# The first unit's lanes with a step per half block, and layer two's first chunk without its meta tokens from the output projection on

## The chip, the cores and the metric

One core of a Trainium2 chip runs the whole program. The metric is the device time of one execution in microseconds. Engines are named as in the profile: PE (TensorE), DVE (VectorE), ACT (ScalarE), POOL (GpSimd) and SP (the queue that issues the loads). Everything is computed in f32.

## The reference

Two layers over 16 meta tokens and 1024 tokens, width 1024. Cut to what matters here:

```python
h = layer_norm(concat([meta, x]))
for i in range(2):
    p_conv, p_swa, p_ret, p_rwkv = split(h @ w_in[i])
    mix = concat([short_conv(p_conv), swa(p_swa), retention(p_ret), rwkv7(p_rwkv)]) @ w_out[i]
    h = layer_norm(ALPHA * h + mix)                      # first norm
    z = causal_dwconv(h @ ffn_w_up[i], ffn_conv_w[i])    # three taps
    u, gate = split(z)
    h = layer_norm(ALPHA * h + (silu(gate) * u) @ ffn_w_down[i])   # second norm
return h[:, N_META:]                                     # the 16 meta tokens are dropped
```

The mixers carry state from the meta tokens to all that follow: attention reads their keys and values in every window, retention and RWKV carry a state. After the mixers of layer two nothing reads the meta tokens but the causal convolution of the feed-forward part, whose three taps reach two tokens back.

## The kernel before

The 1040 tokens are cut into four chunks, the first of 272 tokens (16 meta tokens and 256), the others of 256. A unit u is one chunk in one layer: units 0 to 3 are layer one, 4 to 7 layer two. `chunk_of(u)` gives a unit's first token and its width. Activations are kept transposed, features on partitions and tokens along the free dimension, so the width of a unit is the number of columns of each of its dense products.

A unit has 25 input blocks (`dense`, L852: one weight slot, eight products of 128x128 weights by the unit's columns, summed in one of two PSUM banks that blocks use in turn), 8 output blocks, 44 up blocks and 8 down sums of 22 products each (L1294). PE waits in `bank_free` (L835) until the block two before has been read out by ACT (`evac`) or DVE. SP loads the 792 weight slots of 512 KB in the order of use, five slots deep, each when the slot's last use is over.

Each engine has its own program, written out in Python generators that are advanced in one and the same order on all of them. `alongside(main, *sides)` makes one step of the main program and then one step of each lane; `yield` ends a step. So what stands in a lane's step is issued behind the main part of that step on every engine, and an engine works strictly in its program order. The lanes of a unit are `rwkv(u)` (transposes, scores, a triangular inverse in levels, where PE, DVE's mask at L1708 and ACT's copy at L662 alternate, then the state by tiles) and `side(u)` (retention by tiles with its norm, then sliding-window attention by tiles). From unit 1 on the lanes run beside the up and down products of the unit before. Unit 0 has no unit before it: its lanes run beside its own last input blocks and beside the eight retention input blocks of unit 1 (`project_retention(1)`), and the output projection of unit 0 (`mixer_out(0)`) waits for both lanes. The constants at L112 say after how many steps of the main program the lanes start: RWKV after 12, the input norms of tiles 3 and 4 after 21, retention after 28, attention after 57. In this stretch every block from the 13th on has three steps, of three, three and two products (`steps_after` (2, 5)).

Unit 0's input blocks come in the order of `input_part(0)`: RWKV's seven, retention's eight, the convolution's six, attention's four (sq0, sq1, sk, sv). Two extra products turn sq0, sq1 and sk for the rotary part (tq0, tq1, tk); DVE finishes them in `rotate_swa` and then fills the windows kbuf and vbuf, after which the lane's attention may start. `short_conv` on DVE (L1472 to L1485) runs once cb0 and cb1 are read out.

In retention DVE makes a reciprocal over 544 columns (L1778) and two products. In attention DVE scales and masks the scores (L1793), takes the maximum, ACT makes four exponentials (L733), DVE divides (L1812), PE transposes (L841), ACT copies, PE multiplies by the values (L1239).

The norms of a unit (`residual`, `ln_center`, `ln_normalize` on DVE, `ln_squares`, `ln_affine` on ACT, `ln_mean`, `ln_var` on PE) run beside the blocks of the next unit and have the unit's width.

Of the kernel before, what the change touches and what calls it, by code (L numbers as in the profile page):

```python
# [13 lines left out]
P = 128  # L14
KD = D // P
# [3 lines left out]
HD = 64  # L19
# [51 lines left out]
def input_part(u):  # L71

    return MIX_PART + ([] if u == 1 else RET_PART) + CONV_PART + SWA_PART
# [38 lines left out]
RWKV_START, INPUT_START, SIDE_START, ATTENTION_START = 12, 21, 28, 57  # L112
# [162 lines left out]
def build(nc, x, meta, weights, params, ln_in, ln_rows, consts, tables, out):  # L275
    with ExitStack() as ctx:
# [231 lines left out]
        def _(a):  # L508
            act = a.activation

            def evac(u, name, dst, func=ACT.Copy, bias=None, parts=P):
                i, n = AT[u, name], chunk_of(u)[1]
# [19 lines left out]
            def ln_squares(i):  # L532
                t0, n = chunk_of(i // 2)
# [7 lines left out]
            def ln_affine(i):  # L541
                u, ph = divmod(i, 2)
                t0, n = chunk_of(u)
# [12 lines left out]
            def project(u):  # L556
# [16 lines left out]
                for i, name in enumerate(input_part(u)):  # L573
                    if u == 0 and i >= RWKV_START:
                        yield
                        yield
# [4 lines left out]
                    if u and i == 10:  # L581
                        evac(u - 1, "var1", rstdT[:, :chunk_of(u - 1)[1]], ACT.Sqrt, eps_ln)
# [43 lines left out]
            def project_retention(u):  # L626
# [3 lines left out]
                for name in RET_PART:  # L630
                    yield
                    yield
# [8 lines left out]
            def rwkv(u):  # L641
                for gi, group in enumerate(groups_of(u)):
# [12 lines left out]
                    if u:  # L655
                        yield
# [38 lines left out]
                if u:  # L695
                    yield
# [7 lines left out]
            def side(u):  # L704
# [23 lines left out]
                for i, (j, off, n_) in enumerate(tiles):  # L728
# [8 lines left out]
                    if u:  # L737
                        yield
# [22 lines left out]
            def ffn(u):  # L761
                n = chunk_of(u)[1]
# [17 lines left out]
            def last_norms(u):  # L780
# [5 lines left out]
                evac(u, "var2", rstdT[:, :chunk_of(u)[1]], ACT.Sqrt, eps_ln)  # L786
# [17 lines left out]
            for u in range(NU - 1):  # L804
                if u:
                    rest(ln_squares(2 * u - 1))
                    evac(u - 1, "var2", rstdT[:, :chunk_of(u - 1)[1]], ACT.Sqrt, eps_ln)
# [8 lines left out]
            evac(last, "var1", rstdT[:, :chunk_of(last)[1]], ACT.Sqrt, eps_ln)  # L816
# [8 lines left out]
        def _(pe):  # L825
# [17 lines left out]
            def feature(u, name, pairs, steps_after=()):  # L843
                i, n = AT[u, name], chunk_of(u)[1]
# [23 lines left out]
            def ln_mean(i):  # L868
                u, ph = divmod(i, 2)
                pe.wait_ge(S["dm_sum"], 7 * nth_norm(i) + 7)  # L870
                rest(feature(u, f"mean{ph + 1}", [(c("mean"), xsum[:, nth_norm(i) % 2, :chunk_of(u)[1]])]))

            def ln_var(i):
                u, ph = divmod(i, 2)
                pe.wait_ge(S["ln_sqs"], 7 * nth_norm(i) + 7)
                rest(feature(u, f"var{ph + 1}", [(c("mean"), sqsum[:, :chunk_of(u)[1]])]))
# [19 lines left out]
            def project(u):  # L896
# [12 lines left out]
                for i, name in enumerate(input_part(u)):  # L909
# [7 lines left out]
                    yield from dense(u, name, h, (2, 5) if u == 0 and i >= RWKV_START else ())  # L917
# [103 lines left out]
            def rwkv(u):  # L1021
                first = 1 + ROW["lo"]
                pe.wait_ge(S["smallV"], SMALL_FREED[u, "bo1"])
                for gi, group in enumerate(groups_of(u)):
# [46 lines left out]
                    if u:  # L1071
                        yield
# [1000 lines left out]
```

## Time and profile before

| | |
|---|---|
| median of 3 runs | 3317.38 us (3315.71 to 3317.96) |
| the profiled execution's own time | 3317.04 us |
| its span, first to last instruction | 3315.1 us |
| mean granted clock of TensorE | 0.995 |
| PE busy | 3259.3 us (98%) |
| DVE / ACT / POOL busy | 1346.4 / 867.0 / 34.2 us |
| read from HBM | 427.27 MB, 130 GB/s over the span |

Busy time of PE is that of its matmul records; PEld is the load of weights, which lies beside them. An f32 product is two records. An idle time in the timeline stands in brackets ahead of a group, with what ended it. A granted clock of 1.00 is TensorE's 2.4 GHz, and a stretch's value is a mean over time at either level.

### The profile page before, as it was taken

To read this page: it belongs to the slowest core of one execution; us is meant where nothing else is said; L and a number is where in the kernel's file an instruction comes from. 1 tells how busy PE (TensorE), PEld (TensorE's weight loads), DVE (VectorE), ACT (ScalarE), POOL (GpSimd) and SP (SyncE) were. 2 spreads that over 40 slices of the span, in tenths; PEclk is the share of its full clock that TensorE was granted. 3 is DMA by queue.
4 is the path that set the end of the run, shared out by engine and by line. 5 is a ranking of instruction groups with operands and counts; after the bars stand their busy time and mean duration, and the time that the engine had idled before them with its cause. 6 is when DMAs were issued, how large, how long until landed. Compare 5 with 4: busy or idle time off the path is not lost.

```text
span 3315.1 us, 51403 instructions
## 1 busy us (share of the span) xinstructions
PE 3259.3 (98%) x21648; PEld 2740.6 (83%) x21648; DVE 1346.4 (41%) x3184; ACT 867.0 (26%) x2561; POOL 34.2 (1%) x47
## 2 busy tenths in 40 slices
PE   8989999999999999999999999999999999999998
PEld 6768788888888888878888887888888888888887
DVE  4334452345524454153541534415354153542541
ACT  3223340123402242032330324203242042311320
POOL 0000000000000000000000000000000000000000
PEclk9999999999999999999999999999999999999999
DMA  6134234443344434443334432444334443344443
GB/s 198 58 100 139 91 116 146 147 139 96 127 153 147 134 97 140 153 140 128 103 115 153 140 121 97 140 142 139 127 104 157 149 138 116 121 153 162 154 155 115
DMA packets 128867, 434.79 MB, mean 131 GB/s; under 512 B 13296, under 2 KB 25712, under 8 KB 128384
## 3 DMA queue, kind: packets, MB, share of 16 engines
q1 hardware_dynamic: 127488, 427.32, 39.8%
q8 instruction: 172, 2.82, 0.3%
q0 software_dynamic: 1152, 4.19, 0.3%
q14 instruction: 55, 0.45, 0.0%
HBM read 427.27 MB, written 4.19 MB: 130 GB/s over the span
## 4 chain that ended last, share of the span: by engine, by line
PE 96%; DVE 2%; ACT 1%; issue 0%; DMA 0%; SPq 0%; POOL 0%; DVEq 0%; ACTq 0%
PE psum L847 66%; PE psum L1294 19%; PE psum L841 2%; PE psum L861 2%; PE psum L1095 1%; PE psum L1108 1%; PE psum L1128 1%; PE psum L1239 1%; PE psum L1111 1%; PE psum L1051 0%; PE psum L1221 0%; PE psum L1191 0%; PE psum L1194 0%; DMA con<-in_consts 0%; PE psum L1009 0%
## 5 line engine op out<-in xcount | busy, mean ns | idle before, releaser
L847 PE MATMUL psum<-hT,slots 128*128 128x256 f32 (+1 forms) x8832 | 2012.2, 386 | 11.3 <-DMA con<-in_consts 2.9
L847 PEld LDWEIGHTS psum<-hT,slots 128*128 128x128 f32 x8832 | 1661.6, 190 | 294.1 <-issue 40.5
L1294 PE MATMUL psum<-gT,slots 128*128 128x256 f32 (+1 forms) x2816 | 620.1, 382 | 0.3 <-DVE hT L1398 0.2
L1294 PEld LDWEIGHTS psum<-gT,slots 128*128 128x128 f32 x2816 | 534.3, 190 | 82.7 <-issue 0.5
L1398 DVE SCALAR_TENSOR_TENSOR hT<-hT,psum 128x256 f32<-128x256 f32 (+1 forms) x128 | 54.4, 425 | 622.7 <-PE psum L1294 509.2
L773 ACT ACTIVATE last<-psum 128x2 f32<-128x2 f32 x352 | 60.2, 171 | 910.1 <-PE psum L847 910.0
L847 PE MATMUL psum<-mixT,slots 128*128 128x256 f32 (+1 forms) x1024 | 228.6, 383 | 2.0 <-DVE hT L1398 1.4
L847 PEld LDWEIGHTS psum<-mixT,slots 128*128 128x128 f32 x1024 | 193.6, 190 | 35.8 <-issue 6.6
L1859 DVE TENSOR_SCALAR tmpG<-raw,par 128x256 f32<-128x256 f32 (+1 forms) x176 | 62.7, 356 | 383.4 <-ACT raw L774 383.3
L538 ACT ACTIVATE scr<-hT 128x256 f32<-128x256 f32 (+1 forms) x120 | 47.8, 420 | 593.0 <-DVE hT L1417 569.4
L1859 DVE TENSOR_SCALAR gT<-raw,par 128x256 f32<-128x256 f32 (+1 forms) x176 | 62.4, 355 | 329.1 <-ACT raw L774 329.0
L774 ACT ACTIVATE raw<-psum 128x256 f32<-128x256 f32 (+1 forms) x352 | 134.4, 382 | 0.0
L1863 DVE SCALAR_TENSOR_TENSOR tmpG<-raw,par,tmpG 128x256 f32<-128x256 f32 (+1 forms) x176 | 86.8, 493 | 6.3
L1861 DVE SCALAR_TENSOR_TENSOR tmpG<-raw,par,tmpG 128x256 f32<-128x256 f32 (+1 forms) x176 | 86.8, 493 | 6.3
L1863 DVE SCALAR_TENSOR_TENSOR gT<-raw,par,gT 128x256 f32<-128x256 f32 (+1 forms) x176 | 86.1, 489 | 6.3
L1861 DVE SCALAR_TENSOR_TENSOR gT<-raw,par,gT 128x256 f32<-128x256 f32 (+1 forms) x176 | 86.0, 489 | 6.2
L515 ACT ACTIVATE rows<-psum 128x256 f32<-128x256 f32 (+1 forms) x80 | 31.0, 387 | 218.0 <-PE psum L847 218.0
L1458 DVE TENSOR_TENSOR gT<-rows 128x256 f32<-128x256 f32 (+1 forms) x56 | 24.1, 430 | 137.1 <-ACT rows L565 115.1
L766 ACT ACTIVATE tmpG<-tmpG 128x256 f32<-128x256 f32 (+1 forms) x176 | 74.1, 421 | 12.8 <-DVE tmpG L1863 12.4
L1853 DVE TENSOR_TENSOR gT<-gT,tmpG 128x256 f32<-128x256 f32 (+1 forms) x176 | 74.3, 422 | 1.2
L547 ACT ACTIVATE hT<-hT,par 128x256 f32<-128x256 f32 (+1 forms) x120 | 60.9, 591 | 41.8 <-DVE hT L1437 41.8
L1607 DVE TENSOR_TENSOR rows<-rows,tab 128x256 f32<-128x256 f32 (+1 forms) x48 | 20.5, 426 | 107.0 <-PE psum L847 76.3
(246 smaller groups left out, 2388.0 us busy)
## 6 DMA issues: line engine op xcount, KB each, us to landing
slots<-in_weights SPq DMA_DIRECT2D x792, 512.0 KB, 3.4
hT<-in_x SPq DMA_DIRECT2D x8, 512.0 KB, 5.3
out<-prpt POOLq DMA_DIRECT2D x8, 512.0 KB, 3.0
tab<-in_tables SPq DMA_DIRECT2D x6, 512.0 KB, 4.6
con<-in_consts SPq DMA_DIRECT2D x1, 1562.0 KB, 10.6
tab<-in_tables SPq DMA_DIRECT2D x2, 544.0 KB, 5.7
mixT<-in_ln_rows SPq DMA_DIRECT2D x1, 1024.0 KB, 7.1
par<-in_params SPq DMA_DIRECT2D x2, 386.5 KB, 5.4
```

What stands on the lines that cost most here:

```text
L547: act(hT[:, m, t0:t0 + n], hT[:, m, t0:t0 + n], ACT.Identity, bias=gb[:, KD + m:KD + m + 1], scale=gb[:, m:m + 1]).then_inc(S["ln_hT"], 1)
L766: act(tmpG[:, m % 2, :n], tmpG[:, m % 2, :n], ACT.Silu).then_inc(S["g_silu"], 1)
L773: act(last2[:, u % 2, f, :], psum[:, i % 2, n - 2:n], ACT.Copy)
L774: act(buf[:, 2:2 + n], psum[:, i % 2, :n], ACT.Copy).then_inc(S["evA"], 1)
L841: return pe.transpose(dst, src, ident[:n, :n])
L847: ins = mm(psum[:, i % 2, :n], lhsT, rhs, start=k == 0, stop=k == len(pairs) - 1)
L861: ins = mm(psum[:parts, b, :n], lhsT, rhs, start=k == 0, stop=k == len(pairs) - 1)
L1294: ins = mm(psum[:, i % 2, :n], w[:, e * P:(e + 1) * P], gT[:, k, :n], start=k == 0, stop=k == KF - 1)
L1853: tt(gT[:, m, :n], gT[:, m, :n], tmpG[:, m % 2, :n], ALU.mult).then_inc(S["glu"], 1)
L1859: k = step(ts(y, src[:, 2:2 + n], par[:, w + 2:w + 3], None, ALU.mult))
L1861: k = step(stt(y, src[:, 1:1 + n], par[:, w + 1:w + 2], y, ALU.mult, ALU.add))
L1863: stt(y, src[:, 0:n], par[:, w:w + 1], y, ALU.mult, ALU.add).then_inc(S["fconv"], 1)
```

## The change

`span_of(u, ph)` gives the tokens of a unit that the work after the mixers covers, for the first norm (ph 0) and the second (ph 1). It is the whole chunk but for unit 4, layer two's first: there 14 of the 16 meta tokens are left out from the output projection to the up projection (258 columns remain), all 16 in the down projection and second norm (256). `width(u, name)` picks the width of a block by its name.

In unit 0 the input order becomes RWKV, retention, attention, convolution; tq1 and tk and the filling of the windows follow sv at once instead of standing at the end. A block from the 13th on has two steps of four products each instead of three, in unit 0 and in `project_retention(1)`. The four start constants become 12, 14, 18, 30. Lane steps that only units from 1 on had (`if u: yield`, three places on each engine) unit 0 now has too, one more ahead of RWKV's S2 scores in each of its two groups, one ahead of its last transposes, and one between attention's scores and its transposed probabilities in each tile. In units from 1 on the order of instructions stays as it was.

```diff
+def span_of(u, ph):
+    t0, n = chunk_of(u)
+    skip = (META if ph else META - 2) if u == NCH else 0
+    return t0 + skip, n - skip
+
+def width(u, name):
+    if name[:3] == "out" or name[:2] == "up" or name in ("mean1", "var1"):
+        return span_of(u, 0)[1]
+    return span_of(u, 1)[1] if name[:2] == "dn" or name in ("mean2", "var2") else chunk_of(u)[1]
@@ def input_part(u):
+    if u == 0:
+        return MIX_PART + RET_PART + SWA_PART + CONV_PART
     return MIX_PART + ([] if u == 1 else RET_PART) + CONV_PART + SWA_PART
@@
-RWKV_START, INPUT_START, SIDE_START, ATTENTION_START = 12, 21, 28, 57
+RWKV_START, INPUT_START, SIDE_START, ATTENTION_START = 12, 14, 18, 30
@@ tensor: def project(u)
-                    yield from dense(u, name, h, (2, 5) if u == 0 and i >= RWKV_START else ())
+                    yield from dense(u, name, h, (3,) if u == 0 and i >= RWKV_START else ())
...
-                    yield
-                pe.wait_ge(S["evA"], FREED[AT[u, "sk"]])
-                rest(feature(u, "tq1", [(c("permS"), row("sq1", n))]))
-                rest(feature(u, "tk", [(c("permS"), temp("sk", n))]))
+                    if name == "sv":
+                        pe.wait_ge(S["evA"], FREED[AT[u, "sk"]])
+                        rest(feature(u, "tq1", [(c("permS"), row("sq1", n))]))
+                        rest(feature(u, "tk", [(c("permS"), temp("sk", n))]))
+                    yield
                 yield
@@ tensor: def project_retention(u)
-                    yield from dense(u, name, h_of(u), (2, 5))
+                    yield from dense(u, name, h_of(u), (3,))
@@ tensor, scalar, vector: rwkv(u), side(u)
-                    if u:
-                        yield
+                    yield
@@ scalar, vector: project(u), project_retention(u): one yield less for each block
-                        yield
@@ tensor: def mixer_out(u)
+                first = span_of(u, 0)[0] - chunk_of(u)[0]
-                    rest(dense(u, f"out{m}", [mixT[:, k, :n] for k in range(KD)]))
+                    rest(dense(u, f"out{m}", [mixT[:, k, first:n] for k in range(KD)]))
@@ tensor: def up(u)
-                h = h_of(u)
+                t0, n = span_of(u, 0)
+                h = [hT[:, k, t0:t0 + n] for k in range(KD)]
@@ tensor: def down(u)
-                n = chunk_of(u)[1]
+                n = span_of(u, 1)[1]
+                first = span_of(u, 0)[1] - n
...
-                        ins = mm(psum[:, i % 2, :n], w[:, e * P:(e + 1) * P], gT[:, k, :n], start=k == 0, stop=k == KF - 1)
+                        ins = mm(psum[:, i % 2, :n], w[:, e * P:(e + 1) * P], gT[:, k, first:first + n], start=k == 0, stop=k == KF - 1)
@@ vector: def project(u): rotations and windows
-                    yield
-                rotate_swa(1, row("sq1", n), "tq1")
-                rotate_swa(2, temp("sk", n), "tk")
-                read_out(u, "sv")
...
+                        rotate_swa(1, row("sq1", n), "tq1")
+                        rotate_swa(2, temp("sk", n), "tk")
+                        read_out(u, "sv")
...
@@ residual, ln_center, ln_normalize, ln_squares, ln_affine, ln_mean, ln_var, ffn, up
-                t0, n = chunk_of(u)
+                t0, n = span_of(u, ph)
```

## Rows read from the trace of the kernel before

**Rows 1.** first lines of the page: busy time, share and instructions of each engine

```profile
PE 3259.3 (98%) x21648; PEld 2740.6 (83%) x21648; DVE 1346.4 (41%) x3184; ACT 867.0 (26%) x2561; POOL 34.2 (1%) x47
...
PE psum L847 66%; PE psum L1294 19%; PE psum L841 2%; PE psum L861 2%; PE psum L1095 1%; PE psum L1108 1%; PE psum L1128 1%; PE psum L1239 1%; PE psum L1111 1%; PE psum L1051 0%; PE psum L1221 0%; PE psum L1191 0%; PE psum L1194 0%; DMA con<-in_consts 0%; PE psum L1009 0%
```

**Rows 2.** two stretches of dense work: PE, PEld, DVE, ACT, POOL busy (instructions), clock, DMA

```profile
550.00:600.00 50.00, 50.00 (x220) 41.44 (x219) 4.41 (x10) 0.00 (x0) 0.00 (x0) 1.00 0.44 140
...
1350.00:1400.00 50.00, 50.00 (x233) 44.01 (x233) 4.23 (x10) 0.00 (x0) 0.00 (x0) 1.00 0.50 156
```

**Rows 3.** instruction groups by shape: busy us, mean ns, idle before

```profile
L1294 PE MATMUL psum<-gT,slots 128*128 128x272 f32 x704 | 161.7, 392 | 0.0
...
L847 PE MATMUL psum<-mixT,slots 128*128 128x272 f32 x256 | 59.5, 393 | 0.4 <-DVE hT L1398 0.4
...
L1294 PEld LDWEIGHTS psum<-gT,slots 128*128 128x128 f32 x2816 | 534.3, 190 | 82.7 <-issue 0.5 <-DVE hT L1398 0.5
```

**Rows 4.** waits of PE in 0 to 260 us: total, times, longest

```profile
PE psum L841 <- DVE prpt L1812: 8.5, 3, 4.0
...
PE psum L847 <- DVE gT L1608: 1.6, 2, 1.1
...
PE psum L1095 <- POOL wset L484: 1.4, 1, 1.4
```

**Rows 5.** the first unit's lanes as one window, columns as in group 2

```profile
70.00:230.00 160.00, 141.91 (x1556) 108.56 (x1556) 54.90 (x138) 46.83 (x123) 4.09 (x6) 0.94 0.23 73
```

**Rows 6.** PE in order of time: start us, us, group, idle before

```profile
94.32 1.97 PE L841 MATMUL psum<-con,hT 128*128 128x128 f32 x8 [1.62 <-DVE hT L1381]
...
96.08 4.60 PE L847 MATMUL psum<-hT,slots 128*128 128x272 f32 x10
...
130.51 1.15 PE L1095 MATMUL psum<-wset 64*64 64x64 f32 x32
...
158.71 0.37 PE L1009 MATMUL psum<-Zb,wset 64*64 64x64 f32 x2 [2.92 <-DVE Zb L1665]
...
159.76 4.90 PE L847 MATMUL psum<-hT,slots 128*128 128x272 f32 x10
...
198.84 0.97 PE L1221 MATMUL psum<-kbuf,rows 64*128 64x208 f32 x8
...
199.75 2.42 PE L847 MATMUL psum<-hT,slots 128*128 128x256 f32 x10
...
206.19 1.97 PE L841 MATMUL psum<-con,prpt 128*128 128x128 f32 x8 [4.02 <-DVE prpt L1812]
```

**Rows 7.** VectorE in order of time

```profile
112.59 0.69 DVE L1708 TENSOR_TENSOR wset<-psum,con 128x512 f32<-128x512 f32 x1 [2.82 <-PE psum L1095]
...
149.52 0.06 DVE L1472 MEMSET rows<- 128x2 f32 x1 [8.94 <-ACT gT L515]
...
151.56 0.44 DVE L1485 TENSOR_TENSOR mixT<-mixT,gT 128x272 f32<-128x272 f32 x1
...
153.40 3.54 DVE L1778 RECIPROCAL prpt<-prpt 128x544 f32<-128x544 f32 x1
...
157.73 0.72 DVE L1782 TENSOR_TENSOR mixT<-mixT,prpt 128x544 f32<-128x544 f32 x1
...
178.61 0.50 DVE L1742 SCALAR_TENSOR_TENSOR mixT<-mixT,par,rows 128x272 f32<-128x272 f32 x1 [1.44 <-ACT mixT L699]
...
180.10 0.50 DVE L1744 SCALAR_TENSOR_TENSOR mixT<-mixT,par,rows 128x272 f32<-128x272 f32 x1
...
199.86 1.02 DVE L1793 SCALAR_TENSOR_TENSOR SC<-psum,con 128x832 f32<-128x832 f32 x1 [4.48 <-PE psum L1221]
```

**Rows 8.** ScalarE in order of time

```profile
90.17 1.28 ACT L520 ACT_TABLE_LOAD   x1
...
91.47 0.29 ACT L520 ACTIVATE small<-small,con 128x1 f32<-128x1 f32 x1
...
96.33 2.90 ACT L527 ACTIVATE hT<-psum,ln_in_cols 128x128 f32<-128x128 f32 x8 [3.31 <-PE psum L841]
```

More of the change, by code:

```diff
@@ L581, in project @@
                     if u and i == 10:
-                        evac(u - 1, "var1", rstdT[:, :chunk_of(u - 1)[1]], ACT.Sqrt, eps_ln)
+                        evac(u - 1, "var1", rstdT[:, :span_of(u - 1, 0)[1]], ACT.Sqrt, eps_ln)
                     if name in MIX_PART:
@@ L736, in side @@
                     yield
-                    if u:
-                        yield
+                    yield
                     a.wait_ge(S["a_pt"], nth + 1)
@@ L785, in last_norms @@
                     yield
-                evac(u, "var2", rstdT[:, :chunk_of(u)[1]], ACT.Sqrt, eps_ln)
+                evac(u, "var2", rstdT[:, :span_of(u, 1)[1]], ACT.Sqrt, eps_ln)
                 yield
@@ L806, in _ @@
                     rest(ln_squares(2 * u - 1))
-                    evac(u - 1, "var2", rstdT[:, :chunk_of(u - 1)[1]], ACT.Sqrt, eps_ln)
+                    evac(u - 1, "var2", rstdT[:, :span_of(u - 1, 1)[1]], ACT.Sqrt, eps_ln)
                     ln_affine(2 * u - 1)
@@ L815, in _ @@
             rest(ln_squares(2 * last))
-            evac(last, "var1", rstdT[:, :chunk_of(last)[1]], ACT.Sqrt, eps_ln)
+            evac(last, "var1", rstdT[:, :span_of(last, 0)[1]], ACT.Sqrt, eps_ln)
             ln_affine(2 * last)
@@ L870, in ln_mean @@
                 pe.wait_ge(S["dm_sum"], 7 * nth_norm(i) + 7)
-                rest(feature(u, f"mean{ph + 1}", [(c("mean"), xsum[:, nth_norm(i) % 2, :chunk_of(u)[1]])]))
+                rest(feature(u, f"mean{ph + 1}", [(c("mean"), xsum[:, nth_norm(i) % 2, :span_of(u, ph)[1]])]))
             def ln_var(i):
@@ L875, in ln_var @@
                 pe.wait_ge(S["ln_sqs"], 7 * nth_norm(i) + 7)
-                rest(feature(u, f"var{ph + 1}", [(c("mean"), sqsum[:, :chunk_of(u)[1]])]))
+                rest(feature(u, f"var{ph + 1}", [(c("mean"), sqsum[:, :span_of(u, ph)[1]])]))
             def input_tile(j):
@@ L1070, in rwkv @@
                     yield
-                    if u:
-                        yield
+                    yield
                     pe.wait_ge(S["w_t0"], nth + 1)
@@ L1136, in rwkv @@
                 yield
-                if u:
-                    yield
+                yield
                 pe.wait_ge(S["w_norm"], u + 1)
@@ L1225, in side @@
                     yield
-                    if u:
-                        yield
+                    yield
                     pe.wait_ge(S["a_pn"], nth + 1)
@@ L1560, in project @@
                         yield
-                        yield
                     if i == 2:
@@ L1585, in project @@
                         rotate_swa(0, row("sq0", n), "tq0")
[L1586 to L1596 removed]
+                        rotate_swa(1, row("sq1", n), "tq1")
+                        rotate_swa(2, temp("sk", n), "tk")
+                        read_out(u, "sv")
+                        v.wait_ge(S["a_rope"], 3 * u + 3)
+                        k = step(v.tensor_copy(kbuf[:, :, KPAD:], temp("sk", n)[:, first:].rearrange("p (b s) -> p b s", b=2)))
+                        if c0:
+                            k = step(v.tensor_copy(kbuf[:, :, 0:META], temp("sk", n)[:, None, 0:META].broadcast_to([P, 2, META])))
+                        after(k)
+                        v.tensor_copy(kbuf[:, 1, META:KPAD], kbuf[:, 0, WIN - HD:])
+                        v.tensor_copy(vbuf[:, 1, META:KPAD], vbuf[:, 0, WIN - HD:]).then_inc(S["a_window"], 1)
+                    yield
                 yield
@@ L1697, in rwkv @@
                     yield
-                    if u:
-                        yield
+                    yield
                     v.wait_ge(S["w_s2"], g_ + 1)
@@ L1734, in rwkv @@
                 yield
-                if u:
-                    yield
+                yield
                 yield
@@ L1814, in side @@
                     yield
-                    if u:
-                        yield
+                    yield
                     yield
```

25 lines of the change are left out of this document (8 added, 17 removed).

## The prediction

> **What bounds the kernel now.** I read the engine totals first: PE is busy 98% of the span of 3315.1 us, VectorE (DVE) 41% and ScalarE (ACT) 26%, and the chain that ended last lies mostly on PE's dense products [rows 1]. So time goes away in two ways only: fewer columns through PE, or less time in which PE waits or runs at the lower clock. Next the dense stretches: 50 us hold 220 matmul records of 272 columns or 233 of 256 [rows 2], 0.2273 and 0.2146 us each (an f32 product is two records; a block of eight products is 16). PE is never idle there. Last the waits of PE: after the start-up there is one stretch with many of them, the lanes of unit 0 (70 to 230 us), where PE is busy 141.91 of 160 us, so idle 18.1, at a mean clock of 0.94 [rows 5]. Its largest entries are attention waiting for the normalized probabilities (8.5 us in three waits), rotated features (1.6) and POOL's mask (1.4) [rows 4], the state step (2.9) and the input tile (1.6) [rows 6]. All else that the two parts touch lies in PE's dense stretches.
>
> **Part A, unit 4 without its meta tokens.** Output projection, first norm and up projection go from 272 to 258 columns, down projection and second norm to 256. Counts: of the 256 mixT records of 272 columns half are unit 4's, 128; of the 704 gT records half, 352 [rows 3]; the up projection has 44 blocks x 16 = 704. A column of a record costs (0.2273 - 0.2146)/16 = 0.00079 us [rows 2]. Down: 352 x 0.0127 = 4.5. Output and up: 832 x 14 x 0.00079 = 9.2. Mean and variance products: 8 records, 0.1. Sum 13.8; I take 14.0, since one record more or less in a window of 50 us moves the sum by about 1, so 12.8 to 15. No block of 258 columns is in the trace: its pace lies between that of 256 and of 272 columns, so those 832 records give between 0 and 10.6 us, and I take the linear 9.2, because PE's pace is the same share of the columns at both widths. Narrower operations on DVE and ACT hide under PE and save nothing; a shorter block also shortens the cover of the lanes there, by 6%, and DVE at about half busy has room. The weight queue must bring a slot in 3.43 instead of 3.64 us, which it does in every stretch of 256 columns without a wait of PE [rows 2].
>
> A weight load takes 190 ns [rows 3] and the pace at 256 columns is 214.6 ns. The Trainium skill, TensorE: Matmul & The Clock Gate, section Back-to-back issue gap, says that the spacing of a stream is set by weight load and matmul together. If the load set it, part A would give nothing; the two paces of [rows 2] differ by the columns, so the trace speaks against this here.
>
> **Part B, unit 0's lanes.** A lane advances by one step at each yield of the main program. Before, blocks from the 13th on have three yields, afterwards two: a step then has half a block, 1.96 us at 272 columns or 1.7 to 1.8 at 256, instead of about 1.2 (a block is 16 x 0.2273 = 3.64 us by [rows 2], somewhat more with lane work between). PE's work is the same. I counted lane steps of after as calls 1 to 55 (76 before). RWKV: calls 13 to 53, its first group 13 to 24, second group's transposes 26, scores 27, levels 30 to 39, tiles 41 to 48, last transposes 52. Other lane: input tiles 15 to 18, retention 19 to 29, attention 31 to 46. In before retention and attention lay apart, at 29 to 40 and 58 to 70, attention alone at the end. Now each wait.
>
> Attention. Score products end at 199.8, the chain SC, max, four exponentials and division ends at 206.2, 6.4 us, and PE has 10 records (2.4 us) to do meanwhile [rows 6]. Now it gets three steps instead of two, 5.4 to 5.9 us, with an RWKV step of 1 to 2 us in each. The chain is covered, also with 0.7 us of another lane's DVE work in it [rows 7]: 8.5 us go.
>
> State step. The wait of 2.9 us is DVE's reciprocal (3.54) with its two products, 153.4 to 158.4 [rows 7], queued ahead of the state addition. It moves with retention to call 29, behind the S2 masks. DVE then reaches the mask of the first level 4.9 + 0.7 us after them; PE has two half blocks and one level product (1.15 [rows 6]) from 1.4 us before them on: 1.4 + 4.9 + 0.7 - 3.9 - 1.15 = 1.9 us late. So 2.9 and the 1.0 beside it become 1.9.
>
> Rotated features. They now come in calls 24 to 26 with DVE free, so nearly all of 1.6 goes; 0.2 stays for tk behind ScalarE's copy of sv. The rotations and copies (5 us on DVE) stand ahead of retention's mask, but PE has 16 transposes, retention scores, a half block and the RWKV scores before it needs that: no wait.
>
> POOL's mask. Three steps instead of two stand between scores and first level product, 6 us of PE against a wait of 1.4 after two short ones [rows 4]: it goes.
>
> Short convolution. It takes DVE 2.5 us, 149.5 to 152.0 [rows 7], and now falls in the levels. At cb0 (call 32) the level mask comes 0.5 late. At cb1 (call 38) it stacks: score processing of a full tile 2.8 (two passes of 1.02 [rows 7] and four small ones), convolution 2.6 and mask 0.7 are in order on DVE after scores that end at t, so the mask is there at t + 6.1. PE has a half block and a level product, to t + 3.1, and call 39 has no block at all, the empty yield at project's end. PE waits 3.0 us there. This is the largest new wait.
>
> Input tiles. The first waits for DVE's normalization as before, 1.6 us [rows 6]. The lane has no spare steps ahead of retention any more: the first retention transposes want BX, which ScalarE clears with eight copies in 2.90 us [rows 8], while PE has a half block and a small product. 0.8 late, and 0.2 for the second tile, because Sqrt and Silu now alternate on ScalarE. A change of function shows 1.28 us, with the next instruction 1.30 after its start [rows 8].
>
> ScalarE: Activation LUTs in the Trainium skill, section What ACT_TABLE_LOAD costs, adds a drain of about 1.38 us to each load. By the page the two loads in a row would make input tile and retention start together some 2.7 us later; the row shows no such gap, so that stays out of the sum.
>
> End of lanes. RWKV ends at call 53 of 55. After the last transposes ScalarE and DVE need about 3.4 us, 1.44 of DVE's waiting and products from 178.6 to 180.6 [rows 7], PE has three half blocks, 5.4 us: no wait of the output projection. If the cover were gone it would cost up to 3.4.
>
> Idle in the stretch after: 1.6 + 0.2 + 0.8 + 0.2 + 1.9 + 0.5 + 3.0 + 0.3 (small ones, as before) = 8.5, against 18.1. **Part B gives 9.6 in waits.**
>
> Clock. After the waits of 1.6 and 2.9 us, 10 records take 4.60 and 4.90 us [rows 6], against 2.45 at full pace: about 1.2 instead of 2.4 GHz, 3 us lost each with the lane products beside them. The two long attention waits lost about 1.3 each. After the wait of 1.4 us the clock stayed at 1.00. A mean clock of 0.94 over 160 us [rows 5] bounds the whole loss by 9.6; I count 8.6. Afterwards three waits are of a size that brought the clock down (1.6, 1.9, 3.0), 3 us each: 9. So no gain here, with bounds of +6 (only the first still does it) and -3 (0.8 us too). The Trainium skill, TensorE: Matmul & The Clock Gate, section HAM oscillation, says that the clock falls again when PE goes idle and the next work starts slow; by that rule fewer waits of this size give something back. The trace agrees for the two waits above, and it puts the gain at 0 because as many remain.
>
> **Sum.** 14.0 + 9.6 - 0.1 = 23.5. The profiled execution took 3317.04 us, its span and 1.9 around it; the median is 0.3 above. 3317.04 - 23.5 = 3293.5, with 0.3 for the median 3293.9, so **3294 us**. Own range of this case: part A 12.8 to 15, part B 4 to 16: 3286 to 3301.
>
> **Rivals.**
> 1. Waits change places. Three steps of DVE work in order (score processing, convolution, reciprocal) hit more level masks than I count, and each 3 us wait brings 3 of slow clock. Two more of them eat part B: 14 alone, 3303, within 3301 to 3308. For: DVE works in program order and two lanes now overlap in calls 19 to 46. Against: DVE is busy 54.9 of 160 us [rows 5].
> 2. Nearly all waits hide, the clock falls only at the input tile. Part B gives 16 to 22, 3284. For: the steps hold more PE work than my half block wherever RWKV is in its levels. Against: convolution on top of score processing at the empty yield.
> 3. Slower. The same stacking at nearly every level: 6.1 us of wait and slow clock, one at each of eight or more of the 15 lane steps from 27 to 41. It decides where eight are reached, since 8 x 6.1 = 49 stands against 18.1 + 8.6 that go and 14 of part A: 3325. Only three such places exist by the count of calls.
> 4. Narrow blocks don't pay, because something else than columns sets the pace. Part B alone: 3307.5. Against: [rows 2].
>
> **Chances.** Forecast 0.70, rival 1 0.15, rival 2 0.10, rival 3 0.03, rival 4 0.02. Range: 3286 to 3301 holds 0.70; up to 3303 takes half of rival 1 and down to 3285 a third or so of rival 2. 3285 to 3303. This kernel's measurement can tell about 0.2%, 6.6 us, from no change. Faster by over that: all cases but rival 3 and the edge of rivals 1 and 4, 0.95; within it 0.02; slower 0.03.
>
> **What would show it.** Part A: in unit 4 50 us of up projection hold 231 or 232 records, of down projection 233; the distance from its first output product to its last down product is 13 to 15 us shorter. If it is under 5, 258 columns cost like 272. Part B: waits on prpt from 8.5 to under 1; a wait of about 2 us behind the reciprocal and one of about 3 behind the second convolution, both at L1111 or L1108; PE idle from 70 to 230 us near 8.5. Wrong would be my count of calls if attention still waits over 2 us, my queue on DVE if the two new waits are missing, and my clock if it stays at 1.00 after them.

## The result and the profile after

The changed kernel takes 3284.94 us in the median of four runs (3282.68 to 3285.28), against 3316.94 for the kernel before: 0.9902 of its time, with a 95% interval of 0.9891 to 0.9914. That is 32.0 us less where the sum had 23.5 (3294), just outside the range of 3285 to 3303. By its size it is the case of rival 2, but not by its mechanism. Now and then an execution took from 1.4 to several times as long as the others of its kernel (4592.12 and 10125.35 us of `order_only`, 14930.29 us of the kernel before), and such times are left out of every comparison.

The profiled execution took 3285.28 us, with a span of 3283.1. First line of its page, as in [rows 1]:

```profile
PE 3237.2 (99%) x21648; PEld 2737.6 (83%) x21648; DVE 1343.1 (41%) x3184; ACT 870.8 (27%) x2565; POOL 34.2 (1%) x47
```

The waits of PE up to 260 us (total, times, longest), to be read against [rows 4]. L1120 and L1123 are the level products that were L1108 and L1111, L853 the transposes that were L841:

```profile
PE psum L1123 <- DVE wset L1718: 2.7, 1, 2.7
...
PE psum L1120 <- DVE wset L1718: 2.4, 3, 1.8
...
PE psum L853 <- DVE hT L1394: 1.9, 2, 1.4
...
PE psum L853 <- ACT hT L544: 0.9, 1, 0.9
```

No wait for prpt, rotated features or POOL's mask is left. The first row is the mask behind the second convolution, the second the masks behind the reciprocal (1.85), the first convolution (0.33) and a small step of attention (0.20), then come the two input tiles and ScalarE's copies. Two windows (PE, PEld, DVE, ACT, POOL busy, clock, DMA), against [rows 5] and [rows 2]:

```profile
70.00:230.00 160.00, 151.94 (x1646) 121.09 (x1645) 63.98 (x161) 52.01 (x128) 4.09 (x6) 0.99 0.27 89
...
2150.00:2200.00 50.00, 50.00 (x233) 43.71 (x232) 4.23 (x10) 0.00 (x0) 0.00 (x0) 1.00 0.45 148
```

From 70 to 230 us PE idles 8.06 us instead of 18.1, at a clock of 0.99 instead of 0.94. In unit 4's down products 233 records fill 50 us. From 2080 to 2129 us, in its up projection (128x258), 227 records fill 49 us, which is 231 to 232 in 50, as the prediction named.

Where the 32.0 us of the two spans went can be read off the first output products of units 0, 4 and 5, which cut the program in the same places. PE in order of time (start us, us), before:

```profile
232.87 29.50 PE L847 MATMUL psum<-mixT,slots 128*128 128x272 f32 x128
...
1825.81 3.83 PE L847 MATMUL psum<-mixT,slots 128*128 128x272 f32 x16
...
2239.45 3.62 PE L847 MATMUL psum<-mixT,slots 128*128 128x256 f32 x16
```

and after:

```profile
213.65 29.49 PE L859 MATMUL psum<-mixT,slots 128*128 128x272 f32 x128
...
1806.61 3.64 PE L859 MATMUL psum<-mixT,slots 128*128 128x258 f32 x16
...
2205.83 3.62 PE L859 MATMUL psum<-mixT,slots 128*128 128x256 f32 x16
```

Unit 0's output to unit 4's takes 1592.9 and 1593.0 us, so nothing else moved. Unit 4's output to unit 5's, 413.64 and 399.22: part A gave **14.4 us**. The start to unit 0's output, 232.87 and 213.65: 19.2 us. Of that the first input blocks, ahead of all lanes and unchanged, took 1.1 us more (unit 0's bo products start at 68.22 and 69.30 us), so the lanes gave **20.3 us**. The end of the program took 1.6 us more; the part on the clock shows where. 14.4 + 20.3 - 1.1 - 1.6 = 32.0.

The two new waits stand where DVE's program order puts them. DVE after (start us, us):

```profile
131.41 3.54 DVE L1787 RECIPROCAL prpt<-prpt 128x544 f32<-128x544 f32 x1
...
136.40 0.68 DVE L1718 TENSOR_TENSOR wset<-psum,con 128x512 f32<-128x512 f32 x1
...
160.54 1.02 DVE L1802 SCALAR_TENSOR_TENSOR SC<-psum,con 128x832 f32<-128x832 f32 x1 [3.57 <-PE psum L1232]
...
163.17 0.06 DVE L1485 MEMSET rows<- 128x2 f32 x1
...
165.24 0.44 DVE L1498 TENSOR_TENSOR mixT<-mixT,gT 128x272 f32<-128x272 f32 x1
...
165.59 0.69 DVE L1718 TENSOR_TENSOR wset<-psum,con 128x512 f32<-128x512 f32 x1
```

and PE:

```profile
137.13 0.27 PE L1120 MATMUL psum<-wset 64*64 64x64 f32 x2 [1.85 <-DVE wset L1718]
...
162.45 1.15 PE L1107 MATMUL psum<-wset 64*64 64x64 f32 x32
...
166.33 1.61 PE L1123 MATMUL psum<-wset 64*64 64x64 f32 x32 [2.73 <-DVE wset L1718]
...
167.87 3.14 PE L859 MATMUL psum<-hT,slots 128*128 128x256 f32 x8
...
170.94 1.96 PE L1140 MATMUL psum<-wset 64*64 64x128 f32 x32
```

The first level mask (136.40) follows the reciprocal and its two products, and PE has waited 1.85 us for it. The mask at 165.59 follows score processing from 160.54 and the convolution from 163.17 to 165.6: PE waited 2.73 us. Behind it eight records take 3.14 us instead of 1.8.

The clock by windows of 2 us (columns as above), before, behind the wait of 2.92 us that ended at 158.71:

```profile
158.00:160.00 2.00, 1.29 (x17) 1.17 (x18) 1.15 (x5) 0.00 (x0) 0.00 (x0) 0.61 0.01 4
...
160.00:162.00 2.00, 2.00 (x5) 1.53 (x6) 0.00 (x0) 0.02 (x1) 0.00 (x0) 0.50 0.00 0
...
162.00:164.00 2.00, 2.00 (x5) 1.42 (x5) 0.00 (x0) 0.71 (x3) 0.00 (x0) 0.50 0.42 106
...
164.00:166.00 2.00, 2.00 (x72) 1.41 (x72) 0.00 (x0) 0.00 (x0) 0.00 (x0) 0.69 0.38 156
```

and after, behind the wait of 2.73 us that ended at 166.33:

```profile
166.00:168.00 2.00, 1.67 (x33) 1.55 (x33) 1.55 (x4) 0.02 (x1) 0.00 (x0) 0.70 0.00 0
...
168.00:170.00 2.00, 2.00 (x5) 1.64 (x6) 0.00 (x0) 0.58 (x1) 0.00 (x0) 0.50 0.04 8
...
170.00:172.00 2.00, 2.00 (x24) 1.55 (x25) 0.00 (x0) 0.00 (x0) 0.00 (x0) 0.94 0.00 0
```

PE's busy time in a window times one less the clock is the work time that the lower level cost. Summed over the windows from the bo products to unit 0's output it is 9.6 us before, in four such falls, and 1.6 after, in this one: a gain of **8.0 us**. The 20.3 us of the lanes are thus 10.0 of idle time, 8.0 of clock and 2.2 of neither. What is left of the stretch without idle time and without the clock's loss is 136.7 to 137.3 us in all six profiles with the old lanes (the kernel before, its repeat, `a_only`, `a_late1`, `a_late2`, `order_only`), and 134.4 to 135.0 in the nine with the new lanes in half-block steps and no products added in this stretch.

### The profile page after: what moved, and what is told of

Read it like the earlier page. It is cut to its first block, busy times and chain, and to the rows that moved or that the text cites. A ratio compares the mean times of both kernels' runs of the same rounds, so it can differ in the third digit from the quotient of the medians.

```text
span 3283.1 us, 51407 instructions
## 1 busy us (share of the span) xinstructions
PE 3237.2 (99%) x21648; PEld 2737.6 (83%) x21648; DVE 1343.1 (41%) x3184; ACT 870.8 (27%) x2565; POOL 34.2 (1%) x47
## 4 chain that ended last, share of the span: by engine, by line
PE 97%; DVE 1%; ACT 1%; issue 0%; DMA 0%; SPq 0%; POOL 0%; ACTq 0%; DVEq 0%
PE psum L859 66%; PE psum L1307 19%; PE psum L853 2%; PE psum L873 2%; PE psum L1107 1%; PE psum L1120 1%; PE psum L1064 1%; PE psum L1123 1%; PE psum L1140 1%; PE psum L1249 1%; PE psum L1232 0%; PE psum L1202 0%; PE psum L1205 0%; PE psum L1187 0%; DMA con<-in_consts 0%
## 5 line engine op out<-in xcount | busy, mean ns | idle before, releaser
L859 PE MATMUL psum<-hT,slots 128*128 128x256 f32 (+2 forms) x8832 | 1998.7, 384 | 10.7 <-DMA con<-in_consts 2.9
L859 PE MATMUL psum<-mixT,slots 128*128 128x256 f32 (+2 forms) x1024 | 227.1, 382 | 2.0 <-DVE hT L1411 1.7
L1867 DVE TENSOR_SCALAR tmpG<-raw,par 128x256 f32<-128x256 f32 (+2 forms) x176 | 62.5, 355 | 380.0 <-ACT raw L786 379.7
L1867 DVE TENSOR_SCALAR gT<-raw,par 128x256 f32<-128x256 f32 (+2 forms) x176 | 62.3, 354 | 327.5 <-ACT raw L786 327.4
L786 ACT ACTIVATE raw<-psum 128x256 f32<-128x256 f32 (+2 forms) x352 | 133.9, 380 | 0.0
L1871 DVE SCALAR_TENSOR_TENSOR tmpG<-raw,par,tmpG 128x256 f32<-128x256 f32 (+2 forms) x176 | 86.5, 492 | 6.3
L1869 DVE SCALAR_TENSOR_TENSOR tmpG<-raw,par,tmpG 128x256 f32<-128x256 f32 (+2 forms) x176 | 86.5, 492 | 6.3
L1871 DVE SCALAR_TENSOR_TENSOR gT<-raw,par,gT 128x256 f32<-128x256 f32 (+2 forms) x176 | 85.8, 488 | 6.3
L1869 DVE SCALAR_TENSOR_TENSOR gT<-raw,par,gT 128x256 f32<-128x256 f32 (+2 forms) x176 | 85.7, 487 | 6.3
L778 ACT ACTIVATE tmpG<-tmpG 128x256 f32<-128x256 f32 (+2 forms) x176 | 73.8, 420 | 12.8 <-DVE tmpG L1871 12.4
L1861 DVE TENSOR_TENSOR gT<-gT,tmpG 128x256 f32<-128x256 f32 (+2 forms) x176 | 74.1, 421 | 1.2
L564 ACT ACTIVATE hT<-hT,par 128x256 f32<-128x256 f32 (+2 forms) x120 | 60.7, 589 | 41.5 <-DVE hT L1450 41.5
```

The costliest lines, as they stand in the source:

```text
L564: act(hT[:, m, t0:t0 + n], hT[:, m, t0:t0 + n], ACT.Identity, bias=gb[:, KD + m:KD + m + 1], scale=gb[:, m:m + 1]).then_inc(S["ln_hT"], 1)
L778: act(tmpG[:, m % 2, :n], tmpG[:, m % 2, :n], ACT.Silu).then_inc(S["g_silu"], 1)
L786: act(buf[:, 2:2 + n], psum[:, i % 2, :n], ACT.Copy).then_inc(S["evA"], 1)
L859: ins = mm(psum[:, i % 2, :n], lhsT, rhs, start=k == 0, stop=k == len(pairs) - 1)
L1861: tt(gT[:, m, :n], gT[:, m, :n], tmpG[:, m % 2, :n], ALU.mult).then_inc(S["glu"], 1)
L1867: k = step(ts(y, src[:, 2:2 + n], par[:, w + 2:w + 3], None, ALU.mult))
```

## The experiments

All are variants of one of the two kernels. The kernel before ran beside them on each chip; its medians there lie between 3316.3 and 3318.5 us. Where only one or two times are given, there are no others.

**Each part alone.** `a_only` has the edits with `span_of` and `width` alone, `b_only` all others.

> Part A alone: unit 4's narrower spans, unit 0's lanes as before. By the column count 14.0 us faster than before (12.8 to 15), 3303.0. The rival that 258 columns cost like 272 gives 4.6 us, 3312. Unit 0's stretch keeps its idle 18.1 us from 70 to 230 us and its slow clock. If the clock's fall is a matter of luck between executions and not of the lanes, its mean clock differs from 0.995.

> Part B alone: unit 0's lanes changed, unit 4 with all 272 columns. If the two parts add up: 32.0 - 14.0 = 18 us faster, 3299, with waits of about 8 us from 70 to 230 us and only one short fall of the clock. If part A gave more than the column count (a second effect in unit 4), B alone gives less than 16.

`a_only` took 3299.91 us, 0.995 of before (0.9935 to 0.9965), `b_only` 3298.12, 0.9943 (0.9928 to 0.9958). Unit 4's stretch took 399.22 us in `a_only` and 413.64 in `b_only`: to 0.01 us as in the changed kernel and in the one before. Part A is 14.4 us, neither more nor a third of it. What the profile of `a_only` had beyond that, 2.3 us, lies ahead of unit 0's output (230.54 us instead of 232.87) with all waits as before. The falls of the clock were fewer or shorter: they cost 6.1 us instead of 9.6, and behind the wait of 3.59 us there was none. `b_only` has the waits of the changed kernel, 2.7, 2.4, 1.9 and 0.9.

**The order alone.** `order_only` puts attention's features ahead of the convolution:

```diff
+    if u == 0:
+        return MIX_PART + RET_PART + SWA_PART + CONV_PART
```

> Unit 0's attention features ahead of the convolution, all else as before (three steps a block, old starts). Nothing reads the features earlier, since attention starts at step 57 in any case; the rotated features leave the place where PE waited 1.6 us for them, but DVE's rotations (5 us) now fall beside RWKV's levels or tiles. I expect within 3 us of before. If the order itself were the gain, 5 us or more faster.

It took 3313.11 and 3313.58 us, 3.3 us under before's median of 3316.62. PE's waits for rotated features went from 1.6 to 0.4 us, a wait of 0.9 for the normalized RWKV output came. The 8.5 us of attention stayed. Of the 3.3 us some 2 are the clock's (it cost 7.3 us instead of 9.6). So the order is what lets attention start early, and hardly a gain by itself.

**The half-block step.** `thirds` is the changed kernel with three steps a block:

```diff
-RWKV_START, INPUT_START, SIDE_START, ATTENTION_START = 12, 14, 18, 30
+RWKV_START, INPUT_START, SIDE_START, ATTENTION_START = 12, 14, 18, 36
-                    yield from dense(u, name, h, (3,) if u == 0 and i >= RWKV_START else ())
+                    yield from dense(u, name, h, (2, 5) if u == 0 and i >= RWKV_START else ())
... (the same in project_retention, and a third yield for each block on the other engines)
```

> The changed kernel with three steps a block again (sides' order and added steps kept, attention start 36 instead of 30, because its features come at step 33 then). Tests the half-block step: the waits of the lanes are each for a chain of 2 to 7 us that had 1.96 us of block and now has 1.3. By the cover that a step gives: two to four waits more, 5 to 12 us slower than the changed kernel. If overlap and order alone made the gain: within 2 us of it.

3296.2 us (3295.58 to 3297.09), 11.3 slower than the changed kernel. Its waits from 60 to 240 us:

```profile
PE psum L855 <- DVE prpt L1825: 5.3, 1, 5.3
...
PE psum L1122 <- DVE wset L1722: 2.8, 1, 2.8
...
PE psum L1024 <- DVE wset L1674: 2.2, 2, 1.8
```

From the bo products to unit 0's output it takes 156.24 us, the kernel before 164.65, the changed one 144.35. So some 8 of the 20.3 us come with order, overlap and extra steps, and 12 with the cover that half a block gives. Of these 11.9 us 7.5 are idle time and 3.8 are clock. It fell behind the 5.31 us and behind a wait of 1.80 us for the state, and it stayed at 1.00 behind 2.77 and 1.54 us.

**The queue on DVE.** `long_wait` makes unit 0's reciprocal three times:

```diff
                 k = step(v.reciprocal(rsd[:, :, :n], rsd[:, :, :n]))
+                if u == 0:
+                    for _ in range(2):
+                        after(k)
+                        k = step(v.reciprocal(rsd[:, :, :n], rsd[:, :, :n]))
```

> The changed kernel with unit 0's reciprocal made three times in a row (it then gives the reciprocal again, the result is unchanged): DVE holds the first level's mask 7.1 us longer, so PE's wait of 1.85 us becomes about 9. 7.1 us slower by the queue on DVE alone. Behind so long a wait the clock falls: 2 to 4 us more, 9 to 11 in all. If the clock stays at 1.00 there, only 7.

3294.02 us, 9.1 slower, the lower end of the expected 9 to 11. The level products' wait:

```profile
PE psum L1120 <- DVE wset L1718: 9.3, 2, 9.0
```

1.85 became 9.0, as the queue says, and the clock was 0.50 from 138 to 148 us, during the wait and behind it.

`shift` moves retention and attention one step on, `shift_tight` also drops the empty step at the end of `project` on the three engines:

```diff
-RWKV_START, INPUT_START, SIDE_START, ATTENTION_START = 12, 14, 18, 30
+RWKV_START, INPUT_START, SIDE_START, ATTENTION_START = 12, 14, 19, 31
... (here shift ends)
@@ project(u), after the loop over the blocks (shift_tight)
-                yield
```

> The changed kernel with retention and attention one step later (starts 12, 14, 19, 31). By program order on DVE: the reciprocal falls behind the first level's mask, so its wait of 1.85 us goes; retention no longer waits 0.87 for ScalarE's eight copies; the second convolution comes ahead of the score processing, so the wait of 2.7 shrinks to about 1.5. 3.9 us of waits less, and the fall of the clock behind the 2.7 (1.7 us) with them: 3279.5 to 3281. The rival that DVE's load and not its order makes the waits: they move elsewhere, within 1 us of the changed kernel.

> As the one with retention and attention one step later, and the empty step at the end of unit 0's input projection is gone on all engines, so that half a block of unit 1 (1.8 us) stands between the last two level products. The remaining wait of about 1.5 us goes: 1.5 us faster than that one, 3278 to 3279.5. The end of the lanes has one step less of cover, 3.6 us for 3.4 us of work: if that is too little, up to 1 us comes back at the output projection.

`shift` took 3278.88 us (3278.71 to 3279.56), `shift_tight` **3276.76** (3276.43 to 3276.92), 0.988 of before (0.9862 to 0.9898) and the fastest of all. In `shift` the waits of 1.85 and 0.87 us and those of 0.33 and 0.20 are gone, and the 2.73 became 1.65, behind which the clock stayed at 1.00; it is 0.6 us better than expected. The larger waits left in `shift_tight` from 60 to 240 us:

```profile
PE psum L852 <- DVE hT L1392: 1.9, 2, 1.4
...
PE psum L1020 <- DVE wset L1667: 0.3, 1, 0.3
```

The reciprocal's and both convolutions' waits and the one for ScalarE's copies are gone, so order and not load made them. In the stretch from the bo products to unit 0's output the two took 139.07 and 137.74 us, 5.3 and 6.6 less than the changed kernel. The end of the lanes did not become a wait. `shift_tight` is 1.2 us better than its own expectation reaches; the last norm's wait had no fall of the clock in its profile, and in that of `shift` it had.

**The clock.** The wait of 2.39 us in the last norm stands in all kernels with the same work around it. Behind it PE runs 176 records of 256 columns. The changed kernel:

```profile
3044.40 39.83 PE L859 MATMUL psum<-hT,slots 128*128 128x256 f32 x176 [2.39 <-DVE meanT L1425]
```

and `sparse_ahead` (below), which has the same code there:

```profile
3044.84 38.23 PE L859 MATMUL psum<-hT,slots 128*128 128x256 f32 x176 [2.39 <-DVE meanT L1427]
```

39.83 and 38.23 us. In the first the clock was 0.56 and 0.58 in the two windows of 2 us behind the wait, so some 3.4 us at the lower level, in the second 1.00 throughout. That is the 1.6 us that the end of the changed kernel's profile had lost. I then ran both kernels once more, and the changed one with two and four extra products ahead of block v1:

```diff
                 bank_free(i)
+                for _ in range(4 if (u, name) == (0, "v1") else 0):
+                    mm(psum[:, i % 2, :n], pairs[0][0], pairs[0][1], start=True, stop=True)
```

> The kernel before once more, unchanged, to see whether the falls of the clock are its own or differ between executions. In the first profile it fell behind waits of 1.62, 2.92, 4.02 and 3.59 us and stayed at 1.00 behind the wait of 2.39 us in the last norm. Theory 'moment': whether the clock falls behind a wait of 1.5 to 3 us depends on when the wait lies, so at least one of the waits under 3 us does otherwise here; the two of 3.6 and 4.0 fall again. Theory 'place': all as in the first profile.

> The changed kernel once more, unchanged. In the first profile the clock fell behind the 2.73 us wait (level mask behind the second convolution) and behind the 2.39 us wait of the last norm, not behind 1.37 and 1.85. Theory 'moment': the 2.39 us wait costs its 1.6 us of slow clock or doesn't from one execution to the next, total time 3282.5 or 3285. Theory 'place': the same two falls.

> The changed kernel with two extra products ahead of block v1 of unit 0 (0.9 us; their sums are overwritten): all lanes lie 0.9 us later. 0.9 us slower by work. Theory 'moment': the falls move among the waits of 1.4, 1.85, 2.7 and 2.4 us, the sum of slow time changes by 1.5 to 3 us either way. Theory 'place': the falls are those of the changed kernel's profile.

> As the one with two extra products, with four (1.8 us later). 1.8 us slower by work; by 'moment' another set of waits has a fall behind it, by 'place' the same set.

Times 3317.26, 3283.92, 3287.43 and 3284.07 us. `before_again` showed the falls of the first profile, at the same waits and as long, so "moment" lost there. `after_again` fell behind the same two waits, so "moment" lost there too; it took 1.4 us less, 1.3 of them ahead of the bo products (67.98 us instead of 69.30). `after_late1` fell behind the 2.73 us wait for nearly 7 us instead of 3.4; `after_late2` did not fall there at all, so "place" lost there. Its window at the end of that wait (PE alone busy, clock 1.00):

```profile
166.00:168.00 2.00, 1.00 (x32) 1.00 (x32) 1.93 (x5) 0.00 (x0) 0.00 (x0) 1.00 0.04 16
```

Over all 20 profiles the clock fell behind the 2.39 us wait in 9, behind 2.73 in 9 of 11. The 9 are 9 of the 14 profiles with the new lanes and none of the 6 with the old ones, though the lanes lie 2800 us ahead of that wait; both profiles of the changed kernel had the fall and both of the kernel before had none. Nor does the time since the program's start settle the 2.73: in the changed kernel that wait ended at 166.33 us with a fall, in `wait_longer` (below) at 166.34 without one. Behind the new lanes' first wait (1.37 us in eight profiles without anything put ahead of it, 1.54 in `thirds`) and behind 1.85 (ten) it never fell. And behind the old lanes' 1.62 us it always did. Two more kernels moved that wait, `a_late1` and `a_late2`, part A with the same extra products:

> Part A with the old lanes and two extra products ahead of block v1 of unit 0: its waits of 1.62, 2.92, 4.02 and 3.59 us lie 0.9 us later. Theory 'moment': the clock doesn't fall behind 1.62 here or in the run with four products, as it once didn't behind the 2.7 us wait of the changed kernel. Theory 'place' (what PE did before the wait decides): it falls behind 1.62 again, as in four of four profiles with the old lanes, and never behind the 1.4 and 1.85 of the new ones.

> As the one with two extra products, with four, 1.8 us later. 'Moment': one of the two runs has no fall behind the 1.62 us wait. 'Place': both have it.

3304.68 and 3304.04 us. The clock fell behind 1.62 in both, six of six profiles with the old lanes, for some 7 us and some 3.4. So the length doesn't decide alone (1.62 and not 1.85), nor does the moment as far as these kernels moved it (the wait ended between 94.14 and 97.20 us). What differs is, among other things, ahead of the wait: 2.7 of the old lanes' 4.2 us there are products of the 16-token tile, which use 16 rows. Four kernels put work ahead of the new lanes' 1.37 us wait:

```diff
                     pe.wait_ge(S["w_t0"], nth + 1)
+                    for _ in range(24 if u == 0 and gi == 0 else 0):       # sparse_ahead: 6
+                        scores("k", R0, 0, group[0][1])
@@ or, full_long; rows16 has 16 rows and 16 weight columns of the same; sparse_long as above with 24
+                    for _ in range(9 if u == 0 and gi == 0 else 0):
+                        mm(bank(R3)[:, 0:256], c("mean"), hT[:, 0, 0:256], start=True, stop=True)
```

> The changed kernel with six repeats of the 16-token S2 scores (48 small records, about 1.7 us, the same values again) ahead of the input tile's wait of 1.37 us. Before, such small products stood ahead of the wait of 1.62 us behind which the clock fell; now half a block stands there and it stayed at 1.00. If small products count like idle time for the clock, it falls here: 1.7 us for the products and about 3 for the clock. If the length of the wait alone decides, or the moment, only 1.7.

> The changed kernel with 24 repeats of the 16-token S2 scores (192 small records, the same values again) ahead of the input tile's wait of 1.37 us, some 3.3 us of PE at 16 of 128 rows. The old lanes have 2.7 us of such small products in the 4.2 us ahead of their wait of 1.62. If small products ahead of a wait bring the clock down with it, it falls here, behind 1.37, 3.3 + 3 us slower than the changed kernel. If the wait alone counts: no fall, 3.3 us slower.

> The same place with nine full products of 128x128 by 256 columns (3.9 us, into a free bank, their values are used by nothing) in place of the small ones. Control: no fall of the clock behind the 1.37 us wait by either theory, 3.9 us slower than the changed kernel.

> The changed kernel with nine products of 16 rows and 16 columns of weights by 256 tokens (3.9 us, values used by nothing) ahead of the input tile's wait of 1.37 us: as many instructions and as long as the control with nine full products, behind which the clock stayed at 1.00, and without the 2.6 us gap in issue that the 192 small records brought. If little use of the array ahead of a wait brings the clock down, it falls behind 1.37 here, 3 us more than the control's 3286.6 us of span. If only idle time counts: as the control, within 1.5 us.

`sparse_ahead` took 3283.87 us, its repeats only 0.7 us, and no fall: too little to tell. `sparse_long` took 3292.2 and had the fall, but its many instructions also left PE without any for 2.6 us ahead of the wait, so it doesn't separate the two. `rows16` and `full_long` do. PE in `full_long` (span 3286.6 us), with two windows of 2 us as above:

```profile
81.13 4.05 PE L1087 MATMUL psum<-hT,con 128*128 128x256 f32 x18
...
86.77 1.09 PE L853 MATMUL psum<-con,hT 128*128 128x128 f32 x8 [1.36 <-DVE hT L1396]
...
87.70 2.00 PE L859 MATMUL psum<-hT,slots 128*128 128x272 f32 x8
```

```profile
84.00:86.00 2.00, 1.40 (x14) 0.87 (x12) 0.51 (x4) 0.00 (x0) 0.00 (x0) 1.00 0.09 35
...
86.00:88.00 2.00, 1.23 (x10) 1.19 (x11) 0.71 (x1) 0.10 (x1) 0.00 (x0) 1.00 0.04 8
```

and in `rows16` (span 3286.8):

```profile
79.20 4.05 PE L1087 MATMUL psum<-hT,con 16*16 16x256 f32 x18
...
84.95 1.97 PE L853 MATMUL psum<-con,hT 128*128 128x128 f32 x8 [1.37 <-DVE hT L1396]
...
86.71 3.63 PE L859 MATMUL psum<-hT,slots 128*128 128x272 f32 x8
```

```profile
80.00:84.00 4.00, 3.58 (x24) 1.43 (x21) 0.37 (x3) 0.00 (x0) 0.00 (x0) 0.90 0.40 131
...
84.00:86.00 2.00, 1.05 (x5) 1.05 (x6) 0.86 (x2) 0.00 (x0) 0.00 (x0) 0.50 0.00 0
```

Same number of instructions, same 4.05 us, same wait. With full products the clock is 1.00 before and behind it, and the next eight records take 2.00 us. With 16x16 products the clock is 0.90 from 80 to 84 us: it fell at about 83.2, as the last of them ran and ahead of any idle time, and the eight records take 3.63. From the bo products to unit 0's output `rows16` takes 150.46 us and `full_long` 148.19, 2.3 less where 3 were expected. The totals differ by 0.2 us only, because `full_long` lost 2.0 us ahead of the bo products, where the two are the same. So at this place the clock fell with products in a corner of the array and not with full ones, in one execution of each and on two chips.

`wait_longer` has one more DVE operation ahead of tile 3's normalization, which made the wait 2.35 us with nothing small ahead but the 0.3 us that stand there in all the new kernels:

```diff
+                if j == 3:
+                    for _ in range(1):
+                        k = step(v.reciprocal(rsd[:, :, 0:64], hT[:, 0:2, 0:64]))
+                        after(k)
```

> The changed kernel with one more VectorE reciprocal of 128 columns (about 0.9 us, into a free buffer) ahead of tile 3's normalization: its wait grows from 1.37 to about 2.3 us, with nothing small ahead of it. If the length alone decided with a bound between 1.4 and 1.6 us, the clock falls behind it, as it would behind 1.85, where it never did. By 'moment', the fall comes or not, about as likely; 0.9 us slower, or 0.9 and 1.6 to 3.

3283.57 us, and no fall, behind 2.35 or 2.73.

## Why the prediction missed

**Part A: right.** 14.0 was forecast, 14.4 the measurement, by the column count. Blocks of 258 columns cost as linear interpolation says; rival 4 is out.

**The waits of the old lanes: right.** All of those counted as going went: attention's 8.5, POOL's 1.4, the features' 1.6 (0.16 of it stays, where 0.2 was forecast).

**The new waits: right, each within 0.4 us.** Input tiles 1.4 and 0.55 (1.6 and 0.2), copies 0.87 (0.8), reciprocal 1.85 (1.9), first convolution 0.33 (0.5), second 2.73 (3.0). Idle time after is 8.06 us for 8.5, and waits gave 10.0 for 9.6. Rivals 1 and 3 are out. The count of steps is what carried this: at each, what DVE has queued ahead of the mask.

**The clock: the step that failed.** "Afterwards three waits are of a size that brought the clock down (1.6, 1.9, 3.0), 3 us each: 9. So no gain here." One of the three did, and it cost 1.6 us. By 2 us windows 9.6 us of work time were lost to the lower clock in the old stretch (8.6 were counted) and 1.6 in the new: a gain of 8.0 us. The count beside the quoted sentence gives 8.6 - 9 = -0.4, its text says 0, and the sum has -0.1, which nothing explains. The bound, +6, was too narrow too, because even its best case kept 3 us for the first wait. I read a rule of length out of two waits. One had 2.7 us of the 16-token tile's products in the 4.2 us ahead of it, the other state products, a wait of 0.96 us and six records of a block; ahead of the new 1.37 and 1.85 us half blocks of eight records stand. The pair `rows16` and `full_long` speaks for such a difference at the first wait. That it is what saved the 8 us as a whole is argued, not shown.

**The rest, about 2 us.** 20.3 less 10.0 less 8.0 leaves 2.2, in every profile alike, for which the sum had no term. In before six records behind a lane's products start 1.57 us apart from the next lane piece where the pace gives 1.36; after, eight take 2.03 where it gives 1.82: 0.2 us at each change between block and lane, and there are at most 21 changes fewer. That can have the right size. `thirds`, with three steps a block and the new overlap, keeps all but 0.5 us of it, so it came with order and overlap more than with longer steps. No run separates it further.

**The range.** The 1.1 us at the start are chance of that execution: `after_again`, the same kernel, did not lose them. The 1.6 at the end are the last norm's fall; both profiles of the changed kernel had it and neither of the kernel before, so that it is chance is not shown. The four times of the kernel spread over 2.6 us, and its median lies 0.06 us below the range. The upper side of the range, from rival 1, was never near.

What stays open is what decides behind the last norm's 2.39 us (9 of 20) and behind the 2.73 (9 of 11), and how far small products alone, with how long a wait, make the old lanes' six of six. The 16x16 pair shows the direction, not the amount.

## What to carry to other kernels

Where several lanes share engines in program order, list for each step what is queued on the busiest helper ahead of the mask or copy that PE wants next; this gave every new wait, and moving retention and attention by one step took four of them away and shortened the largest. Price a wait of PE at its length, and add the clock's fall as a chance and not as a fact: in these profiles it came behind all waits of 4.02 us and more, behind 3.59 in five of six, behind 2.39 in 9 of 20, and behind 1.62 in six of six where small products stood ahead. A narrower last part of a kernel (tokens that nothing reads any more) is worth its columns, to a few per cent, when PE is the bound.

## What was not expected of the hardware

Nine 16x16 products of 256 columns took as long as nine full ones (4.05 us), and as the last of them ran the granted clock fell from 2.4 to 1.2 GHz, before PE was idle. The same wait of 2.39 us in the same code was followed by the lower level for some 3.4 us in 9 of 20 profiled executions and cost 1.5 to 1.7 us when it was. The first 64 records of a program, the same code in all, took from 16.4 to 18.0 us in different executions, and the granted clock doesn't explain it: from 18 to 24 us PE made 20 records in the kernel before, where the clock reads 0.72, and 15 in the changed one, where it reads 1.00. In the 11 profiles where the clock reads 0.72 to 0.77 there the 64 records took 16.4 to 16.6 us, in the 9 where it reads 1.00 from 17.0 to 18.0. There 15 records in 6 us are a pace of 0.40 us, nearer to the 0.46 of records at the lower level behind the waits than to the 0.23 at the higher one. So there the reading may be wrong and not the pace; no run shows it. This is where the 1.1 us at the start went, and no run says why.
